# Swapping two VectorE steps in the expert loop of a one-core MoE kernel: the second lane's weight copy moves right behind the gated rows

## What is computed

```python
def swiglu(h, wg, wu, wd):
    return (jax.nn.silu(h @ wg) * (h @ wu)) @ wd
...
    def expert_block(args):
        tok, rw, e = args
        xs = hp[tok]
        y = swiglu(xs, w_gate_e[e], w_up_e[e], w_down_e[e])
        return (y.astype(jnp.float32) * rw[:, None]).astype(hf.dtype)
...
    routed = jnp.zeros((T + 1, D), hf.dtype).at[row_tok].add(y.reshape(R, D))[:T]
```

## Time and profile before

| | before |
|---|---|
| median of 3 runs | 2647.73 us |
| the profiled execution: its time, its span | 2645.02 us, 2643.2 us |
| TensorE busy | 2504.4 us (95%) |
| VectorE busy | 1600.5 us (61%) |
| ScalarE busy | 792.5 us (30%) |
| GpSimd busy | 1284.3 us (49%) |
| granted TensorE clock, mean | 0.978 |
| HBM read and written | 569.55 MB, 127.02 MB |

### The profile page before, as it was taken

One profiled execution on the slowest core, in us unless ns is written; L12 is line 12 of the kernel. 1 busy time (PEld: TensorE's weight loads), 2 busy tenths in 40 slices (PEclk: granted clock), 3 DMA queues, 4 the chain that ended last, 5 costly groups with the idle time before them and its releaser, 6 DMA issues.

```text
span 2643.2 us, 45878 instructions
## 1 busy us (share of the span) xinstructions
PE 2504.4 (95%) x12502; PEld 1161.4 (44%) x12503; DVE 1600.5 (61%) x2547; ACT 792.5 (30%) x1403; POOL 1284.3 (49%) x943
## 2 busy tenths in 40 slices
PE   6999999999999999999999999999999999999870
PEld 2588888887694333333333333333333333333220
DVE  3567777776664555555556565555655555555446
ACT  3455554554311222222222222222222222222114
POOL 0012212222143666666556666666666676666550
PEclk8999999999999999999999999999999999999995
DMA  9622122114536776989999998999999978889948
GB/s 366 245 81 80 64 72 80 72 72 160 199 121 243 235 226 193 317 294 347 355 355 321 352 322 282 355 313 356 309 324 326 353 228 282 283 280 346 357 126 360
DMA packets 147951, 664.25 MB, mean 251 GB/s; under 512 B 37779, under 2 KB 38828, under 8 KB 95302
## 3 DMA queue, kind: packets, MB, share of 16 engines
q1 hardware_dynamic: 89958, 528.96, 51.4%
q0 software_dynamic: 57952, 134.77, 21.6%
HBM read 569.55 MB, written 127.02 MB: 264 GB/s over the span
## 4 chain that ended last, share of the span: by engine, by line
PE 79%; DMA 15%; DVE 2%; SPq 2%; issue 1%; ACT 1%; DVEq 0%; POOLq 0%; ACTq 0%
PE PB L1668 32%; PE PB L1675 17%; DMA arena<-in_w_up_e 13%; PE PB L1560 3%; PE PB L1561 3%; PE PB L1565 3%; PE PB L1488 2%; PE PB L1375 2%; PE PB L1681 2%; PE PB L1378 1%; PE PB L1602 1%; PE PB L1476 1%; PE PB L1477 1%; PE PB L1480 1%; DMA arena<-acc_tab 1%
## 5 line engine op out<-in xcount | busy, mean ns | idle before, releaser
L1668 PE MATMUL PB<-arena 128*64 x2528 | 1113.1, 593 | 1.3 <-issue 1.3
L1669 PE MATMUL PB<-arena 128*64 128x512 f32 x2528 | 1113.1, 593 | 0.0
L601 POOL DMA_INDIRECT arena<-h_tab,rec x644 | 781.6, 1214 | 244.6 <-issue 214.1
L1668 PEld LDWEIGHTS PB<-arena 128*64 128x64 f32 x2528 | 346.7, 137 | 727.3 <-issue 727.3
L1675 PE MATMUL PB<-arena 128*64 x1264 | 609.3, 605 | 3.3 <-issue 3.3
L1676 PE MATMUL PB<-arena 128*64 128x512 f32 x1264 | 609.3, 605 | 0.0
L635 POOL DMA_INDIRECT acc_tab<-arena,rec x157 | 358.7, 2285 | 426.7 <-DMA acc_tab<-arena,rec 245.6
L1239 DVE COPY arena<-arena 128x4096 f32 x160 | 369.6, 2310 | 135.9 <-DMA arena<-in_w_up_e 68.7
L592 POOL DMA_INDIRECT rec_tab<-recs,posi x128 | 132.5, 1035 | 605.3 <-DVE recs L1046 568.4
L1278 DVE SCALAR_TENSOR_TENSOR arena<-PB,RW,arena 128x512 f32<-128x512 f32 x314 | 221.3, 747 | 244.8 <-PE PB L1676 134.3
L1669 PEld LDWEIGHTS PB<-arena 128*64 128x64 f32 x2528 | 346.7, 137 | 0.0
(11 more groups left out here) (310 smaller groups left out, 2647.8 us busy)
## 6 DMA issues: line engine op xcount, KB each, us to landing
arena<-in_w_gate_e SPq DMA_DIRECT2D x128, 1024.0 KB
arena<-in_w_up_e SPq DMA_DIRECT2D x128, 1024.0 KB
arena<-in_w_down_e SPq DMA_DIRECT2D x128, 1024.0 KB
arena<-in_ada_w SPq DMA_DIRECT2D x24, 1024.0 KB, 10.4
arena<-in_x SPq DMA_DIRECT2D x32, 512.0 KB, 3.4
acc_tab<-arena SPq DMA_DIRECT2D x32, 512.0 KB, 2.6
arena<-acc_tab SPq DMA_DIRECT2D x6, 2048.0 KB, 22.6
arena<-h_tab,rec POOLq DMA_INDIRECT x644
```

Of the source, the lines that this page charges most:

```text
L601: g.indirect_dma_start(xg[n % AHEAD][:, a * F:(a + 1) * F], None, h2_tab.rearrange("t (a n) -> (t a) n", a=4), bass.IndirectOffsetOnAxis(a ...
L1668: mm(B[7][0:SUB, :], xTm[n % 2][:, k, 0:SUB], wa(k), start=(k == 0), stop=(k == KD - 1))
L1669: last = mm(B[7][SUB:P, :], xTm[n % 2][:, k, SUB:P], WBG[n % 2][:, k], start=(k == 0), stop=(k == KD - 1))
```

## The change

Two steps of VectorE's loop body change places, and one of them also moves to another unit. Before, iteration b transposed the rows of unit b+2 right behind `gated()`, and copied the weights of unit b+3 at the end. After, iteration b copies the weights of unit b+2 right behind `gated()`, and transposes the rows of unit b+3 at the end. The step ahead of the loop that copied unit 2's weights becomes one that transposes unit 2's rows, and SP's wait behind the loop counts one copy fewer. Both are still one operation each, on VectorE.

```diff
@@ sync engine, behind the loop
-            sp.wait_ge(s["v_cg"], nu + 2)
+            sp.wait_ge(s["v_cg"], nu + 1)
@@ vector engine
             gated()
-            gu_copy(2, 2)
+            v.wait_ge(s["xg_r2"], 64)
+            rows_T(2)
             with v.Fori(0, MAXU // UNROLL) as q:
...
                             v.wait_ge(s["eg_done"], b + 2)
                             gated()
-                            m = n + 2
-                            v.wait_ge(s[f"xg_r{m % AHEAD}"], (q * (UNROLL // AHEAD) + (m // AHEAD + 1)) * 64)
-                            settle(v)
-                            rows_T(m)
+                            gu_copy(n + 2, v.snap(b + 2))
                             v.wait_ge(s["y_done"], b + 1)
                             v.wait_ge(s["added"], b * 16 + 16)
                             settle(v)
...
-                            gu_copy(n + 1, v.snap(b + 3))
+                            m = n + 3
+                            v.wait_ge(s[f"xg_r{m % AHEAD}"], (q * (UNROLL // AHEAD) + (m // AHEAD + 1)) * 64)
+                            settle(v)
+                            rows_T(m)
```

## The result

The changed kernel took 2766.3 us (median of 4 runs, 2764.54 to 2767.51) against 2645.49 (median of 4, 2642.9 to 2650.1) of the kernel before beside it: a ratio of 1.046, 95% interval 1.0446 to 1.0474. Its profiled execution took 2764.54 us, span 2762.3, which is 119.5 us more than that of before.

A forecast was written before the change was run, and what follows sets the result against it. TensorE was taken as the bound, waiting for nobody in the usual unit. 0.96 us more in each of 156 units made 150, less 27 of stalls: +123 on 2645, so 2768 us; range 2725 to 2840.

The forecast's parts named there:

- What bounds the kernel: In the usual unit of 10.82 us TensorE waits for nobody; the moved copy must be done for its matmul at 3.32.
- Register work, 1.75: On VectorE's sequencer, the copy's register work starts with `gated()`, not ahead of it, so the copy starts 1.75 us behind.
- the first rival: Copy in time behind `gated()`: starts at 0.45, ready at 2.89, only the stalls change, 2618 us; chance 0.06, wholly or nearly.
- Copy, 2.29, and release, 0.15: VectorE's weight copy takes 2.29 us and ends at 4.04; TensorE's first gate matmul follows 0.15 later, at 4.19.
- 7.55 from the first gate matmul to the next `gated()`: TensorE's stretch after its idle time takes 7.55 us, against 7.50 in the run-on, making the unit 11.74, 0.92 more.
- POOL, 0.04 per unit: The copy at its new place meets POOL's gathers more often and lasts 0.04 us longer per unit.
- the rival in which POOL holds the copy up: The copy waits out the rest of a gather and starts 0.6 us later each time: 2855 us; chance 0.03.
- Stalls, -27: TensorE's 26.6 us of stalls, from copies late for weights, go with later use and a slower TensorE.
- Transposition at nothing: VectorE's transposition of 2.02 us at its new place, a whole unit ahead, costs nothing, waits for gathers included.
- TensorE's busy share, put at 92%: Sign in the profile after: TensorE's busy share in the steady stretch falls from all of it to about 92%.
- 2988 for a fall in every unit: Clock rival: TensorE's idle time lowers its clock, 1.4 us in each of 156 units, 218 more; chance 0.06, some or all units.

The follow-up runs named there:

- `hoist_both`: The changed kernel with both table loads of the weight copy put ahead of the wait for the silu; 2658.13 us, ratio 0.9975 to the kernel before, 0.9966 when repeated.
- `hoist_one`: The changed kernel with only the load of the slot's place put ahead of the wait for the silu; 2687.19 us, ratio 1.0081 to the kernel before.
- `before_light`: The kernel before, loading only a quarter of each expert's down weights and leaving the rest of the slot stale; 2650.4 us, ratio 0.9973 to the kernel before.
- `half_copy`: The changed kernel with the loop's copy moving only the gate half, stale second-lane up weights being used; 2658.46 us, ratio 0.9978 to the kernel before.

## Why the prediction was right

**What bounds the kernel.** Right. TensorE in its own order was the bound, and the deadline for the second lane's weights was the first gate matmul.

**Register work, 1.75.** Measured 1.77, and the chain shows it begin with `gated()`, not ahead of it. `hoist_both` and `hoist_one` show that this term decided, against a copy of 2.29: with both loads ahead the path is 0.45, which is the number that the first rival had given for this case.

**Copy, 2.29, and release, 0.15.** The copy is 2.29; from its end to the matmul it is 4.20 - 1.77 - 2.29 = 0.14.

**7.55 from the first gate matmul to the next `gated()`.** 1021.90 - 1014.36 = 7.54. The unit of 11.74 is exact.

**POOL, 0.04 per unit.** Mis-sized, and the reason given for it was wrong. The copy took 2.295 us on the mean, from this row of the page, so the term is 0:

```profile
L1239 DVE COPY arena<-arena 128x4096 f32 x159 | 365.0, 2295 | 186.3 <-issue 171.6
```

That is 6 us too many in the sum. The prediction had the copy fall among the gathers more often. It falls into POOL's pause, between the last gather and a scatter that waits for index copies behind the copy. In the loop of before, 71 of 158 copies began while a POOL instruction ran, and 117 POOL instructions began during a copy; in the changed kernel it is 9 of 157, and none. That they miss each other, by 0.25 us in the unit above, is luck as far as the prediction goes. So the rival in which POOL holds the copy up was hardly put to the test here. By the Trainium skill (SBUF — State Buffer, Who interferes with whom), of a VectorE copy in a two-port mode and a GpSimd instruction the one that comes first holds the shared pair of ports for its whole instruction, and the other waits. The traces show such waits in both directions, but not for a whole gather; the last section has the numbers.

**Stalls, -27.** Mis-sized: 23.8 came back of 30.5, by the account above. Both halves of the mechanism have a share: the later use alone (`hoist_both`) leaves 16.7 of 25.9 to 30.5, and the slower TensorE of the change 6.7. In the sum, 6 us too many in the cost of POOL and 3 too many in the gain partly cancel, which is luck, and the remainder is 0.92 x 156 = 143.5 against 144.4.

**Transposition at nothing.** Right: no transposition waited for a gather, and 4.27 us of VectorE's time is left behind it. TensorE's busy share, put at 92%, is 94%: of the 0.92 us more per unit only 0.71 shows as idle time.

**The rivals.** The clock stayed at 1.00 in the steady stretch, so 0.7 us of idle time in each unit costs no clock here. (The prediction's 2988 for a fall in every unit should read 2768 + 218 = 2986, on the base of its 2841.) The first rival's own case, the copy in time, was then built as `hoist_both`: its path of 0.45 was as priced, its gain of 27 us was 8.8 and 9.3, since the order alone doesn't take the stalls away.

## What to carry to other kernels

A step that is moved directly behind a semaphore wait takes its register loads with it: here two table loads and their operations made the path 1.77 us instead of 0.45, and without them all of the 144 us was gone. Put the loads ahead of the wait, and compare the path with the deadline of the engine that waits for it; beyond the deadline each microsecond costs a microsecond per unit.
When transfers are late, look first at what the issuing engine waits for, not at the bytes: a chain of one load after the other can be too slow with bandwidth left. And a short gap of one engine may be the time in which another gets its work started; taking it away isn't free.

## What had not been expected of the hardware

- VectorE's copy and POOL's indirect DMA instructions do hold each other up. Outside of copies a gather takes 0.99 to 1.06 us and a scatter 1.57 to 1.64, in the loops of before and after. In the unit of `hoist_both` above, the copy starts 0.45 us into a gather, is not held, and the gather ends 0.11 us behind the copy, at 2.85. That holds for every copy that starts within 0.54 us of a gather's start in the traces with the full copy: the gather ends 0.12 to 0.13 behind the copy. A copy that starts 0.60 to 0.70 into a gather is itself the longer one, 2.40 to 2.52 us, and the gather keeps its length; from 0.54 to 0.60 both cases occur. One of the second kind from the kernel before, at 0.56:

```profile
1301.86 1.00 POOL L601 DMA_INDIRECT arena<-h_tab,rec  x1 [0.30 <-issue]
1302.42 2.53 DVE L1239 COPY arena<-arena 128x4096 f32 x1 [8.27 <-DMA arena<-in_w_up_e]
```

- So the copy loses at most 0.25 us by it and is 2.25 to 2.33 on the mean in all kernels with the full copy, while POOL's means swing with where its instructions fall: a gather takes 1214 ns, 1041 in the changed kernel (the row below), 1386 in `hoist_both`, where 121 of 158 copies begin in a POOL instruction. In `before_light` it takes 1036, but there 140 of 158 scatters begin during a copy and take 3155 instead of 2285. In `hoist_both` this cost the steady unit nothing.

```profile
L601 POOL DMA_INDIRECT arena<-h_tab,rec x644 | 670.4, 1041 | 244.5 <-issue 215.6
```

- Leaving out three quarters of the down weights' loads saved 0.27% of the time, three quarters of the up weights' 1%.
- A register load of 0.31 us took 1.34 once in `half_copy`.
